# A two-block network on one Trainium2 core: orders of work moved in attention, mixer and experts' first gathers, and one more home for a chunk of experts' weights

## The reference, cut to what matters

```python
def mlstm_mixer(x, w_in, b_gates, conv_w, conv_b, norm_g, w_out):
    qk, v, o_pre, gates = jnp.split(x @ w_in, [2 * D, 3 * D, 4 * D], axis=-1)
    qk = jax.nn.silu(causal_conv(qk, conv_w, conv_b))
    ...                      # scores of q and k, weights, values, denominators
    h = head_norm(h, norm_g, H) * jax.nn.sigmoid(o_pre)
    return h @ w_out

def grouped_moe(x, w_router, w1, w3, w2):
    ...                      # gates: two of 16 experts for each row
    for e in range(N_EXPERTS):
        h = jax.nn.silu(t @ w1[e]) * (t @ w3[e])
        y = y + gates[:, e:e + 1] * (h @ w2[e])

def second_block(...):       # for each of two layers
    parts = rms_and_modulate(x) @ w_in[l]       # queries, keys, values, gates
    ...                      # rms and rotation of each head, two attentions
    x = x + gt1 * (mixed @ w_out[l])
    x = x + gt2 * (square(relu(h2 @ w_ff1[l])) @ w_ff2[l])
```

## Time and profile before

| | us |
|---|---|
| median of 3 runs | 1484.76 |
| lowest, highest | 1483.83, 1485.95 |
| profiled execution | 1485.66 |
| its span on the core | 1483.8 |
| PE busy in the span | 1443.6 |
| DVE busy | 910.2 |
| ACT busy | 626.7 |

### The profile page before, as it was taken

How to read it: one execution, slowest core, us unless ns; L and a number is a source line. 1 busy time by engine, 2 the same in 40 slices (tenths; PEclk the granted TensorE clock), 3 DMA queues, 4 the chain that set the end, 5 groups by cost and what they waited for, 6 DMA issues and landing times.

```text
span 1483.8 us, 20474 instructions
## 1 busy us (share of the span) xinstructions
PE 1443.6 (97%) x8383; PEld 1068.5 (72%) x8383; DVE 910.2 (61%) x1549; ACT 626.7 (42%) x1004; POOL 40.8 (3%) x39
## 2 busy tenths in 40 slices
PE   9999999989999999999799999999999999999998
PEld 7885444436888544443578897999988898799997
DVE  4986111118787611111799888997968976775555
ACT  6453211115334321211555655454456566465443
POOL 0000000000000000000210000000002000000000
PEclk9999999999999999999899999999999999999999
DMA  9897999998467899999665463899955533445540
GB/s 379 314 365 301 426 427 426 427 426 329 166 247 297 331 424 427 427 426 426 247 231 184 181 232 142 335 369 352 357 182 187 197 123 125 151 170 193 179 168 29
DMA packets 59062, 420.17 MB, mean 283 GB/s; under 512 B 6657, under 2 KB 6721, under 8 KB 8658
## 3 DMA queue, kind: packets, MB, share of 16 engines
q1 hardware_dynamic: 58322, 417.17, 71.5%
q0 software_dynamic: 640, 1.61, 0.4%
HBM read 417.71 MB, written 1.05 MB: 282 GB/s over the span
## 4 chain that ended last, share of the span: by engine, by line
PE 80%; DVE 11%; DMA 4%; ACT 3%; issue 1%; SPq 0%; DVEq 0%; ACTq 0%
PE ps L869 78%; DVE lo L2111 2%; DMA AR<-in_moe 2%; DMA raw<-in_moe 2%; DVE AR L2104 2%; PE ps L1520 1%; DMA AR<-in_wgu 1%; DVE AR L2101 1%; PE ps L1491 1%; ACT AR L2011 1%; PE ps L1244 1%; DVE TINY L2104 1%; DVE ACC L2104 0%; PE ps L991 0%; PE ps L1001 0%
## 5 line engine op out<-in xcount | busy, mean ns | idle before, releaser
L2111 DVE TENSOR_TENSOR lo<-raw,hi 128x1024 fp32r<-128x1024 f32 x296 | 359.4, 1237 | 97.7 <-ACT hi L1661 97.0
L1661 ACT ACTIVATE hi<-raw 128x1024 fp32r<-128x1024 f32 x296 | 306.2, 1056 | 183.3 <-PE ps L869 178.1
L869 PE MATMUL ps<-T,hi 128*128 128x256 f32 x1792 | 323.8, 283 | 1.4 <-DVE lo L2111 0.6
L869 PE MATMUL ps<-hi,T 128*128 128x512 f32 x896 | 285.8, 396 | 1.0 <-DVE lo L2111 0.6
L869 PEld LDWEIGHTS ps<-T,hi 128*128 128x128 f32 x1792 | 277.1, 189 | 10.0 <-issue 5.1
L869 PE MATMUL ps<-T,lo 128*128 128x256 f32 x896 | 249.2, 280 | 0.0
L869 PEld LDWEIGHTS ps<-hi,T 128*128 128x128 f32 x896 | 169.0, 189 | 38.0 <-DVE lo L2111 2.1
L869 PE MATMUL ps<-lo,T 128*128 128x512 f32 x448 | 172.8, 390 | 0.0
L869 PEld LDWEIGHTS ps<-T,lo 128*128 128x128 f32 x896 | 169.2, 189 | 0.3 <-DVE lo L2111 0.3
L869 PE MATMUL ps<-hi,AF 128*128 128x512 f32 x512 | 163.3, 391 | 0.0
L2104 DVE SCALAR_TENSOR_TENSOR AR<-AR,ps 128x512 f32<-128x512 f32 x52 | 35.4, 684 | 192.0 <-PE ps L869 104.8
(11 more groups left out here) (247 smaller groups left out, 1730.5 us busy)
## 6 DMA issues: line engine op xcount, KB each, us to landing
raw<-in_moe SPq DMA_DIRECT2D x76, 1024.0 KB, 17.1
raw<-in_b_ff SPq DMA_DIRECT2D x64, 1024.0 KB, 5.3
AR<-in_moe SPq DMA_DIRECT2D x59, 1024.0 KB, 17.1
raw<-in_ada SPq DMA_DIRECT2D x48, 1024.0 KB, 6.7
ring<-in_moe SPq DMA_DIRECT2D x45, 1024.0 KB, 15.8
raw<-in_b_in SPq DMA_DIRECT2D x24, 1024.0 KB, 6.0
raw<-in_b_gate SPq DMA_DIRECT2D x16, 1024.0 KB, 4.8
ACC<-in_moe SPq DMA_DIRECT2D x12, 1024.0 KB, 20.2
```

Of the source, the lines that this page charges most:

```text
L869: return e.matmul(o, l, r, start=a, stop=z, skip_group_check=True)
L1661: e.activation(hi[n % NC][:, :], raw[place[c]][:, 1024 * half:1024 * half + 1024], ACT.Copy).then_inc(*to("hi", "hi", n))
L2111: tt(lo[n % NC][:, :], r, hi[n % NC][:, :], SUB).then_inc(*to("lo", "lo", n))
```

## The change

Five edits:

1. `walk_moe`: gather 2 of group 0 moves from before pair 0 to behind its first `up` job, beside gather 3. All four gathers of group 1 move to pair 1: two at s = 2, two at s = 4.
2. `walk_mlstm`: `pace` begins 0, 0, 1 in place of 0, 1, 2. Scores 3 now stand after the third `og` job, three values after the fourth, (1,1), den and the first stats after the fifth, the other stats and the scale after the sixth, the norms after the seventh.
3. `walk_attention`: a block with two parts is turned one job later.
4. A lent home 13 is `TF[:, 2048:4096]`. In each experts' layer chunk 11 lives there, and only that chunk; the ring opens at chunks 12 to 16 and `ACC` at 17, each one later than before.
5. SP's wait for home 13 is that of the ring.

```diff
@@ walk_moe
-    for k in range(3):
+    for k in range(2):
         yield ("gather", 0, k)
...
             if p == 0:
-                yield ("gather", 0, 3)
+                for k in (2, 3):
+                    yield ("gather", 0, k)
                 yield ("sum_turn", key)
...
         if p < 6:
-            for k, at in enumerate((1, 4) if p else (2, 3)):
+            for k, at in enumerate((2, 2, 4, 4) if p == 1 else (1, 4) if p else ()):
                 if s == at:
-                    yield ("gather", p // 2 + 1, 2 * (p % 2) + k)
+                    yield ("gather", p // 2 + 1, k if p == 1 else 2 * (p % 2) + k)
@@ walk_mlstm
-    pace = iter((0, 1, 2) + 13 * (3,))
+    pace = iter((0, 0, 1) + 13 * (3,))
@@ walk_attention
-        turns.append([LAG, n])
+        turns.append([LAG + len(SEGS[n][0]) - 1, n])
@@ two_block_kernel
-        raw += [x[:, :] for x in ring] + [ar(0, 2048)]
+        raw += [x[:, :] for x in ring] + [ar(0, 2048), TF[:, 2048:4096]]
@@ sync_program, load
-                    elif 6 < q < 12:
+                    elif 6 < q < 12 or q == 13:
                         w.wait_ge(*after(*ring_free(i)))
@@ build
-            ring = tuple((7 + n, 11 + n, 80) for n in range(5))
-            spare[i] = [(p, at + c, at + last) for p, c, last in (*early, *ring, (0, 16, 95))]
+            ring = ((13, 11, 11), *((7 + n, 12 + n, 80) for n in range(5)))
+            spare[i] = [(p, at + c, at + last) for p, c, last in (*early, *ring, (0, 17, 95))]
```

## The result

The changed kernel takes 1495.69 us (median of 4 runs, 1494.92 to 1496.88) against 1485.36 for the kernel before on the same chip (4 runs, 1483.83 to 1486.03). The ratio is 1.0072, 95% interval 1.0054 to 1.0089: slower by 10.3 us, above the predicted range, whose upper end was 1489.4.

A forecast was written before the change was run, and what follows sets the result against it. PE's own work was taken to bound mixers and attention, the 427 GB/s transfers the experts. Attention 0, experts 0 +0.3, mixer +2.75, clock +1.4, experts 1 -1.8 make +2.65 on 1484.76: 1487.4 us, range 1482.8 to 1489.4.

The forecast's parts named there:

- 1.6 said: Layer 1's mixer: PE waits 1.6 us in a new place, before the first values, for DVE's weighted scores.
- 3.0 said: Layer 1's mixer: values start 3.0 us later, at 447.9, behind DVE's accumulation, split and weighting.
- 0.3 said: Layer 0's experts: +0.3 us, since gather 3 and DVE's normalised rows come later and SP's wait for line 2207 stays.
- The reading of the 1.18 us as a landing: End of layer 1's experts: PE's 1.18 us wait at 701.52, labelled issue, was read as a chunk landing.
- It stays 10.6 long: Layer 1's mixer: the DVE, ACT, DVE chain from den to the first turn keeps its 10.6 us.
- the prediction had 3.4: Layer 1's mixer: PE is ready at 464.0, the turn comes at 467.4, so PE waits 3.4 us.
- With one split of weights inside before and one after: Layer 1's mixer: the chain from den to the turn holds one split of weights in the old order and the new.
- A wait of 1.29 us left the granted clock at 1.00: Layer 1's mixer, old wait before scores 3: 1.29 us of waiting left PE's clock at 2.4 GHz.
- den starts 3.0 us later: Layer 1's mixer: den moves by 3.0 us to 456.9, with the same work between values and the last denominators.
- 1.4 us said: Layer 1's mixer, behind the turn: half clock after the new 3.4 us wait costs 1.4 us, 0 as the other end.
- The wait of 0.25 us: Layer 1's mixer, behind the turn: PE's next wait of 0.25 us goes, as the split before DVE's part is done.
- 1.8 us said: Layer 1's experts: one more chunk in flight fills the stream's hole between 506 and 526 us, winning 1.8 us.

The follow-up runs named there:

- `home6_late`: The changed kernel with the old mixer pace, and layer 0's home 6 opening for chunk 24 in place of 19: 1481.91 us, ratio 0.9972 against the kernel before.
- `norms_kept`: Kernel before with pace 0, 0, 1, 3, 3, 2, so both norms stand together after the seventh `og` job: 1491.16 us, ratio 1.0043.
- `pace_fills`: Kernel before with edit 2, plus unread matmuls in PE's two new waits, 8 before the first values and 24 before the turn: 1492.16 us, ratio 1.005.
- `pace_only`: Kernel before with edit 2 alone (pace 0, 0, 1): 1495.34 us, ratio 1.0072.
- `rest_only`: The changed kernel with the old pace, that is edits 1, 3, 4 and 5: 1484.9 us, ratio 1.0004 against the kernel before.
- `kept_clock`: `home6_late` plus unread matmuls in three PE waits: 27 in layer 0's modulation, 11 and 5 before attention's first turns: 1481.45 us, ratio 0.9971.
- `attn_fills`: `home6_late` plus 11 and 5 unread matmuls before the first turns of attention 0 and 1 alone: 1481.56 us, ratio 0.9974.
- `gathers_only`: Kernel before with edit 1 alone, the new places of the experts' gathers, no new home: 1485.39 us, ratio 0.9998.
- `branch_later`: `home6_late` with PE's flag load and branch over the overflow code two jobs later in each experts' layer: 1483.13 us in one run.
- `no_branch`: `home6_late` without PE's flag load and branch over the overflow code in both experts' layers: 1479.87 us, ratio 0.9966.

## Why the prediction was wrong

**Right.** Edit 2 has the sign and the places: the wait before scores 3 is gone, PE waits 1.77 us for the weighting before the values (1.6 said), values start later by 3.8, of which 0.65 were there already at DVE's last convolution (440.51 in place of 439.86), so 3.1 are the mixer's (3.0 said). Behind the turn's wait the clock is at 0.50. Layer 0 lost 0.3 us, counted from SP's first load there (330.01 - 118.47 = 211.54 against 211.23; 0.3 said), the wait of SP for line 2207 stayed (7.5 us of the 8.69 for the three issues, 5.6 before), and `home6_late` shows that it was the cause of the hole. Edits 1 and 3 measure nothing. The reading of the 1.18 us as a landing was right, on thinner evidence than the table above.

**The step that failed first: "It stays 10.6 long".** The chain from den to the turn grew by 2.69 us, and PE waited 6.0 us for it where the prediction had 3.4. The list of side steps in the section on the kernel before has "an empty one" between the scale and the norms; the mixer of layer 1 has none, that is the other mixer's list. So with three steps a job the sixth job's group is second norm_stats, scale, norm 0, and norm 1 with the gated heads falls behind the seventh job; the section on the change, which has both norms after the seventh, is wrong by the same step. "With one split of weights inside before and one after" missed this one, between the norms: 1.06 us on ACT and 1.23 us on DVE and their handing over. `norms_kept` brings back exactly 10.58.

**"A wait of 1.29 us left the granted clock at 1.00", and no price on the wait of 1.6.** The sum has "den starts 3.0 us later", the same as values. The stretch in between grew by 3.42 us, all of it the half clock's, which `pace_fills` gives back to the hundredths (9.04 between values and the den copy, 8.99 before). The prediction prices the clock behind the new wait of 3.4 us and names no price for the one of 1.6; the only row near it, 1.29 us, had none. The price was not bounded from the other side, by the 2.65 us of the earlier trace rows. Two prices stood in the trace, and the 1.6 us were between them.

**The clock behind the turn: 1.4 us said, 2.80 measured for the stretch to SP's load,** 2.15 of it up to the next turn (14.53 in place of 12.38), and 0.44 a new wait at 495.76. The wait of 0.25 us did go, as predicted; the new one is not the clock's, `pace_fills` has it too. Against `pace_fills`, where this part takes 481.93 - 470.08 = 11.85 us, the half clock cost 2.7 us in the changed kernel and 1.6 in `pace_only` (13.44), where it came back sooner. So 1.4 us is near the lower of two measured prices, and the difference is the chance of the execution.

**Layer 1's experts: 1.8 us said, 0.7 measured.** The hole of 38 GB/s over 20 us was filled as predicted. In `rest_only`, which has this edit without the mixer's, the load of the last chunk before the 1.18 us lands 0.5 us sooner only. Counted from SP's first load behind the mixer to the first `down` job of pair 7 the edit is worth 0.7 us there too (208.88 in place of 209.56), and the other three kernels with this layer 1 (`home6_late`, `kept_clock`, `attn_fills`) take 208.80 to 208.93. In that time 88.4 MB were moved in `rest_only` and 88.3 in the changed kernel (423 GB/s), against 87.8 before (419 GB/s). The 0.5 MB more are 1.3 us of the stream, about what is missing from the 1.8; it looks as if loads issued behind the last chunk had got further by the time it landed. What lets them is not settled: no view here divides the time by transfer engine, and no run took these later loads away. The filled hole of layer 0 was worth 2.8 us of a computed 3.7.

Summed by the measured terms: 0.65 (start and experts 0) + 12.0 (mixer with its clock) - 0.7 (experts 1) = 11.95, less 2.5 that this execution happened to get back further on, mostly by the clock behind the old waits: 9.4 of span, and 10.3 between the medians.

## What to carry to other kernels

A step moved behind one more job is also moved against every other step: write down, for the new order, what stands between each two links of the chain that ends last, on each engine, from the code of this very list. A new wait on TensorE has two prices, its length and the half clock behind it, and the length doesn't settle the second; where the trace has one wait that didn't lower the clock and a longer one that did, the price for one in between goes into the sum or at least into the range. And a stream of loads with a hole is cured at the load on which its queue waits: give that load another home or another place in the order, before adding homes.

## What the runs showed of the hardware

- The same length of wait has not the same effect on TensorE's clock. Behind 1.77 and 1.78 us (after, `pace_only`) PE ran some 5 us at 0.50 while fully busy; behind 1.29 us it stayed at 1.00; behind 2.65 us, at attention's first turn, it was halved before (transposes 1.97 us) and not after (1.09 us), nor in `rest_only`, `gathers_only`, `home6_late`, `pace_fills` and `branch_later` (1.09 us each). So 1.77 us halved it where 2.65 us mostly did not, and the clock price that the prediction took from the earlier trace rows was that of one execution. The Trainium skill (TensorE: Matmul & The Clock Gate, "HAM oscillation — how this bites in real kernels") charges half of the throttled stretch. The trace agrees in the second stretch: the windows from 447 to 460 stand at 0.89, 0.50 and 0.88, which is 0.11 x 3 + 0.50 x 5 + 0.12 x 5 = 3.43 us of lost clock, and the stretch grew by 3.42.
- Unread matmuls in a wait keep the clock (`pace_fills`, 3.2 us less than `pace_only`), but only pay where PE's own work follows. Where the next thing is again a wait for DVE (`kept_clock`), the wait grows by what was won.
- Where PE loads a flag into a register and branches it has a gap of 1.3 to 1.8 us in each layer of experts (over the kernels that have the branch in its old place), and none in `no_branch`; taking it away won 0.3 us in layer 0 and 1.3 in layer 1. The Trainium skill (Advanced Engine Details and Errata, "Control Flow Timing") gives 108 ns for a compare and branch alone; no run here parts the load and its wait from the branch.
- The 16 transfer engines together move 427 GB/s without a hole (window 170 to 295), and the 1 MB chunk that the first `down` job of pair 7 waits for lands 18.4 to 20.9 us behind its issue in either layer, so some eight chunks of 2.46 us are in flight (an estimate from these numbers).
